# A four-layer streaming encoder on one core: a third output tile's partial products beside the last mixer and the memory job, and a new order of the side products

## The reference: what is computed

```python
h = _rmsnorm(x, norm_g[i])
u = h @ (w_in_a, w_in_b, w_in_c)[kind][j]
mix_u, mq, gate = u[..., :n_mix], u[..., n_mix:n_mix + MEM_W], u[..., n_mix + MEM_W:]
br, st = _mixer_a(...)   # or _mixer_b, _mixer_c
mo = _mem_attend(mq, mem_k[i], mem_v[i])
y = jnp.concatenate([br, mo], axis=-1) * jax.nn.silu(gate)
x = x + y @ w_out[i]
```

## Time and profile before

| | |
|---|---|
| median of three runs | 2914.63 us (2906.01 to 2914.76) |
| the profiled execution | 2914.56 us, span 2912.8 us |
| instructions | 46710, of them 18936 matmuls |
| TensorE busy with matmuls | 2741.2 us |
| its weight loads, beside them | 2572.5 us |
| VectorE and ScalarE | 1322.6 and 1320.6 us |
| GpSimd | 733.3 us |
| mean granted clock of TensorE | 0.971 of full speed |

### The profile page before, as it was taken

How to read it: one execution, slowest core, us unless ns; L and a number is a source line. 1 busy time by engine, 2 the same in 40 slices (tenths; PEclk the granted TensorE clock), 3 DMA queues, 4 the chain that set the end, 5 groups by cost and what they waited for, 6 DMA issues and landing times.

```text
span 2912.8 us, 46710 instructions
## 1 busy us (share of the span) xinstructions
PE 2741.2 (94%) x18936; PEld 2572.5 (88%) x18936; DVE 1322.6 (45%) x3225; ACT 1320.6 (45%) x2833; POOL 733.3 (25%) x408
## 2 busy tenths in 40 slices
PE   7999999989999999979999989999899999999897
PEld 5989999879989999969999878888799999999886
DVE  4035555563215566664425245555613045555642
ACT  4244444442325555552334356666523244444532
POOL 0222222235122222232521122222051222222313
PEclk9999999999999999989999999999899999999998
DMA  4111111115111121114211000000242111111111
GB/s 150 54 50 54 54 47 47 50 32 185 61 40 63 56 70 52 59 39 149 81 59 39 25 27 12 11 12 3 76 147 68 47 47 47 57 47 46 56 68 74
DMA packets 58629, 171.98 MB, mean 59 GB/s; under 512 B 6768, under 2 KB 15472, under 8 KB 57904
## 3 DMA queue, kind: packets, MB, share of 16 engines
q1 hardware_dynamic: 58416, 169.01, 16.8%
HBM read 135.06 MB, written 33.92 MB: 58 GB/s over the span
## 4 chain that ended last, share of the span: by engine, by line
PE 79%; ACT 9%; DVE 8%; issue 3%; DMA 0%; POOL 0%; SPq 0%; DVEq 0%; ACTq 0%
PE acc L1849 39%; PE acc L1939 10%; PE acc L1797 7%; PE turned L1898 6%; PE scores L1882 5%; PE scores L1730 4%; ACT prob L1243 4%; PE turned L1730 2%; PE scores L1871 2%; DVE prob L1534 2%; PE scores L1706 1%; DVE pt_split L1563 1%; DVE y_sb L1592 1%; ACT pt_split L1255 1%; ACT prob L1246 1%
## 5 line engine op out<-in xcount | busy, mean ns | idle before, releaser
L1849 PE MATMUL acc<-h_split,w_hi 128*128 128x352 f32 (+2 forms) x5112 | 960.6, 330 | 28.7 <-ACT w_rest L1096 14.3
L1849 PEld LDWEIGHTS acc<-h_split,w_hi 128*128 128x128 f32 x5112 | 835.0, 191 | 59.2 <-ACT w_rest L1096 16.9
L1628 POOL TENSOR_TENSOR w_lo<-w_raw,w_hi 128x1024 fp32r<-128x1024 f32 (+2 forms) x154 | 333.6, 2168 | 1559.5 <-ACT w_hi L1149 1559.5
L1563 DVE TENSOR_TENSOR pt_split<-turned,pt_split 128x512 fp32r<-128x512 f32 (+4 forms) x564 | 303.2, 552 | 552.4 <-ACT pt_split L1255 551.7
L1534 DVE CUSTOM_DVE_ANT_0 prob<-scores,bias 128x256 f32<-128x256 f32 (+9 forms) x576 | 338.4, 633 | 416.6 <-PE scores L1882 390.8
L1939 PE MATMUL acc<-pt_split,v_split 128*64 128x256 f32 (+5 forms) x3486 | 479.0, 273 | 25.9 <-ACT pt_split L1255 8.0
L1849 PE MATMUL acc<-h_split,w_lo 128*128 128x352 f32 (+2 forms) x2556 | 495.5, 324 | 0.0
L1243 ACT ACTIVATE prob<-prob,stat 128x256 f32<-128x256 f32 (+9 forms) x468 | 303.7, 650 | 305.7 <-DVE stat L1534 305.7
L1939 PEld LDWEIGHTS acc<-pt_split,v_split 128*64 128x64 f32 (+1 forms) x3486 | 389.1, 154 | 42.1 <-ACT pt_split L1255 15.5
L1849 PEld LDWEIGHTS acc<-h_split,w_lo 128*128 128x128 f32 x2556 | 426.0, 190 | 0.0
L1255 ACT ACTIVATE pt_split<-turned 128x512 fp32r<-128x512 f32 (+4 forms) x564 | 261.7, 482 | 242.4 <-PE turned L1898 241.4
(11 more groups left out here) (142 smaller groups left out, 2818.9 us busy)
## 6 DMA issues: line engine op xcount, KB each, us to landing
w_raw<-w SPq DMA_DIRECT2D x132, 512.0 KB, 3.7
x_scr<-y_sb SPq DMA_DIRECT2D x24, 528.0 KB, 5.5
y_sb<-x_scr SPq DMA_DIRECT2D x24, 528.0 KB, 9.1
y_sb<-x_in SPq DMA_DIRECT2D x16, 528.0 KB, 11.7
mw_raw<-w SPq DMA_DIRECT2D x16, 512.0 KB, 9.2
bias<-rel_in SPq DMA_DIRECT2D x24, 320.0 KB, 4.2
raw<-kcache SPq DMA_DIRECT2D x18, 256.0 KB, 3.9
v_cache<-vcache SPq DMA_DIRECT2D x18, 256.0 KB, 3.9
```

What stands on the lines that cost most here:

```text
L1563: ins = dve.tensor_tensor(pt[0:rows, chunk.p % 2, 1, c0:c0 + n], t_ps[chunk.a % 2][0:rows, c0:c0 + n], pt[0:rows, chunk.p % 2, 0, c0:c0 + ...
L1628: pool.tensor_tensor(w_lo[:, n % 2, 0:wide], w_raw[:, n % 2, 0:wide], w_hi[:, n % 2, 0:wide].bitcast(F32), ALU.subtract).then_inc(wlo_made ...
L1849: ins = pe.matmul(acc[s.bank][:, 0:s.cols], w[ws][:, 128 * k:128 * k + 128], x(xs, k), start=(k, y) == products[0], stop=(k, y) == product ...
```

## The change

- **First memory job of layers 0, 1 and 3.** Two of the first mixer's query sides, not none, stand before the first transposes (`ahead` 2), and the five units get 1, 1, 2, 2, 1 of the other seven sides (`BESIDE_FIRST`), where it was 2, 1, 3, 2, 1.
- **Last mixer of A and B.** The three memory-query sides stand in the units as 1, 0, 2, 0, 0 (`BESIDE_LAST`), where it was 1, 1, 1, 0, 0.
- **Output tiles.** Three of them, not two, get partial sums (`OUT_FIRST`), so nine thirds. Two of these stand already in the last mixer's decoded unit, the other seven as 2, 1, 1, 2, 1 (A) or 1, 2, 1, 2, 1 (B) in the memory job's five units. The first tile's thirds leave out k tiles 5 and 7, so 18 matmuls; those of the others leave out 7. Inside a third all high-half activations of the k tiles come first, then the low ones; tile 5's products come last.
- **Tails.** The missing products (5 and 7 for the first tile, 7 for the others) are made from four slots, filled by ScalarE from `w_hi` and `w_lo` (`tailcopy`, both halves) behind the last third of each tile. GpSimd's subtraction for them goes. `before_last` has nine groups instead of six.
- **Gated tiles' copies.** In the last mixer, tiles 6 and 0 are copied in its fourth unit, behind the first transposes; 1 in chunk 2 of that unit; 2 and 3 in its decoded unit, behind the first transposes; 4 behind the memory job's first normalisation. Tile 4's low half is VectorE's now.
- **Output phase.** The pair are tiles 3 and 4; it waits for each weight where it is used first, and begins with all passes of the first weight. Squares 0 and 1 stand before the next weights' splits. `outtile` is left for 5, 6 and 7; the next layer's memory preparation stands behind 5 (one quarter) and 6 (two quarters).
- **Latent mixers' short unit** (two chunks, three sides): one side stands in chunk 0 and two in chunk 1, where it was two and one. Chunk 1's transposes and the second tile of the next unit's scores stand between.

```diff
+BESIDE_LAST = (1, 0, 2, 0, 0)
+
+BESIDE_FIRST = (1, 1, 2, 2, 1)
+
...
-OUT_POOL = (6, 0, 1, 2, 3, 4)
-
-OUT_PARTS = {"A": (1, 1, 1, 2, 1), "B": (0, 2, 1, 2, 1)}
+OUT_POOL = (6, 0, 1, 2, 3)
+
+OUT_PARTS = {"A": (0, 0, 0, 0, 2, 2, 1, 1, 2, 1), "B": (0, 0, 0, 0, 2, 1, 2, 1, 2, 1)}
+
+OUT_FIRST = 3
+
+TAILS = ((5, 7), (7,), (7,))
+TAIL_SLOTS = {(0, 5): 0, (0, 7): 1, (1, 7): 2, (2, 7): 3}
...
     def out_sides(self, layer, weights):
-        return [self.side(w, KT - 1, "opart", a, cols, f, layer, c, 3, 1)
+        return [self.side(w, KT - len(TAILS[f]), "opart", a, cols, f, layer, c, 3, 1)
                 for f, w in enumerate(weights) for c, (a, cols) in enumerate(THIRDS)]
...
+        if s.what == "opart" and part == parts - 1 and s.chunk == s.chunks - 1:
+            self.order.append(("tailcopy", s))
...
             if nxt.kind == "M" and j.kind != "M":
-                count, ahead = (count[0] + ahead, *count[1:]), 0
+                count, ahead = BESIDE_LAST, 0
+            if j.kind == "M" and nxt.kind in "AB":
+                count, ahead = BESIDE_FIRST, 2
...
-        ahead = 2 if gates else AHEAD[jobs[1].kind]
+        ahead = 2 if out or gates else AHEAD[jobs[1].kind]
...
-            if out and u.job is jobs[-1]:
-                if u is u.job.units[0]:
-                    listed = self.out_sides(u.job.layer, out)
-                count, at = OUT_PARTS[KINDS[u.job.layer]], u.job.units.index(u)
-                sides = listed[sum(count[:at]):sum(count[:at + 1])]
+            if out and i >= len(units) - 10:
+                count, at = OUT_PARTS[KINDS[u.job.layer]], i - len(units) + 10
+                if at == 4:
+                    parts_of_out = self.out_sides(u.job.layer, out)
+                if at >= 4:
+                    sides = parts_of_out[sum(count[:at]):sum(count[:at + 1])]
...
-            if out and u is jobs[-2].units[2]:
-                self.early_y(u.job.layer, (6, 0))
-            if out and u is jobs[-2].units[3]:
-                self.early_y(u.job.layer, (1, 2))
-            if out and u is jobs[-2].units[4]:
-                self.early_y(u.job.layer, (3, 4))
...
+            if k < OUT_FIRST:
...
+        early = {}
+        if out and job is jobs[-2]:
+            early = {3: {2: (1,)}}.get(at, {})
...
+            if n == 2 and len(sides) == 3 and job.kind == "C":
+                parts[i > 0].append((s, 0, 1))
+                continue
...
+                if out and job is jobs[-2] and at >= 3:
+                    self.early_y(job.layer, (6, 0) if at == 3 else (2, 3))
...
+                if out and job is jobs[-2] and at == 4:
+                    self.early_y(job.layer, (4,))
...
+            self.early_y(job.layer, early.get(c, ()))
...
-            p.stream(memory[:1] + mixers + memory[1:], out=x["out"][:2])
+            p.stream(memory[:1] + mixers + memory[1:], out=x["out"][:OUT_FIRST])
...
-        first = 0 if kind == "C" else 2
+        first = 0 if kind == "C" else OUT_FIRST
         p.phase("out", layer=layer, weights=x["out"], first=first)
+        p.order += [("square", layer, f) for f in range(min(first, 2))]
         p.used(*x["out"][first:first + 2])
-        p.order += [("square", layer, f) for f in range(first + 2)]
+        p.order += [("square", layer, f) for f in range(min(first, 2), first + 2)]
...
             p.order.append(("square", layer, f))
-            t = f - 3 if first else f - 2
-            if t < 4 and layer < DEPTH - 1:
-                p.order += [("msplit", layer + 1, t), ("mnorm", layer + 1, 2 * t), ("mnorm", layer + 1, 2 * t + 1)]
+            for t in {5: (1,), 6: (2, 3)}.get(f, ()) if first else (f - 2,):
+                if t < 4 and layer < DEPTH - 1:
+                    p.order += [("msplit", layer + 1, t), ("mnorm", layer + 1, 2 * t), ("mnorm", layer + 1, 2 * t + 1)]
...
+    wt_hi = sbuf("w_tail_hi", [4, 128], F32R, at=qo_at)
+    wt_lo = sbuf("w_tail_lo", [4, 128], F32R, at=qo_at + 2048)
...
+                    act.wait_ge(*tail_made.upto(n - 2))
...
-                if n in tail_weights:
-                    act.activation(wt_hi[:, tail_weights[n], :], w_raw[:, n % 2, 128 * (KT - 1):128 * KT],
-                                   ACT.Copy).then_inc(tail_hi.mark(n), 1)
...
+            elif name == "tailcopy":
+                s = item[1]
+                act.wait_ge(*operand_lo.upto(plan.last_job[s.job].n, 1))
+                act.wait_ge(*whi_made.upto(s.weight))
+                act.wait_ge(*wlo_made.upto(s.weight))
+                for k in TAILS[s.dst]:
+                    slot, cols = TAIL_SLOTS[s.dst, k], slice(128 * k, 128 * k + 128)
+                    act.activation(wt_hi[:, slot, :], w_hi[:, s.weight % 2, cols].bitcast(F32), ACT.Copy).then_inc(
+                        tail_made.mark(s.weight), 1)
+                    act.activation(wt_lo[:, slot, :], w_lo[:, s.weight % 2, cols].bitcast(F32), ACT.Copy).then_inc(
+                        tail_made.mark(s.weight), 1)
...
-                if n in tail_weights:
-                    f, tail = tail_weights[n], slice(128 * (KT - 1), 128 * KT)
-                    pool.wait_ge(*tail_hi.upto(n))
-                    pool.tensor_tensor(wt_lo[:, f, :], w_raw[:, n % 2, tail], wt_hi[:, f, :].bitcast(F32),
-                                       ALU.subtract).then_inc(tail_lo.mark(n), 1)
...
-            for w in weights:
-                pe.wait_ge(*whi_made.upto(w))
             passes = ((0, 0), (1, 0), (0, 1))
             for k in ks:
                 if k == ks[-1] and before_last is not None:
                     before_last()
                 pe.wait_ge(*hi_ready(k))
                 listed = [(y, i) for y in range(3) for i in range(2)]
-                if k == ks[-1]:
-                    pe.wait_ge(*lo_ready(k))
+                if k == ks[-1] or k == ks[0] and before_last is not None:
                     listed.sort(key=lambda yi: yi[1])
                 for y, i in listed:
                     (ws, xs), w = passes[y], weights[i]
                     if xs == 1 and i == 0:
                         pe.wait_ge(*lo_ready(k))
+                    if k == ks[0] and y == 0:
+                        pe.wait_ge(*whi_made.upto(w))
                     if ws == 1 and k == ks[0]:
                         pe.wait_ge(*wlo_made.upto(w))
...
-                        pe.wait_ge(*tail_lo.upto(more["weights"][1]))
-                        for f in range(2):
+                        pe.wait_ge(*tail_made.upto(more["weights"][first - 1]))
+                        for f in range(first):
...
+                                products = [(k, y) for k in TAILS[f] for y in range(3)]
+                                for k, y in products:
+                                    ws, xs = PASSES[y]
+                                    ins = pe.matmul(acc[i % 2][:, 0:n], (wt_hi, wt_lo)[ws][:, TAIL_SLOTS[f, k], :],
+                                                    h_v[:, xs, k, a:a + n], start=(k, y) == products[0],
+                                                    stop=(k, y) == products[-1])
...
+                    if KINDS[layer] != "C" and f == OUT_FIRST + 2 and c < 2:
+                        pe.wait_ge(*out_added.upto(layer, OUT_FIRST - 1, 1 + c))
...
-                    products = [(k, y) for k in OUT_ORDER["A"][:-1] for y in range(3)]
+                    products = [(k, y) for ys in ((0, 2), (1,)) for k in OUT_ORDER["A"] if k not in (5, 7) for y in ys]
+                    products += [(5, y) for y in range(3) if s.k_tiles == KT - 1]
...
-                    if s.what == "opart" and s.chunk == s.dst == 0:
+                    if s.what == "opart" and s.chunk == 0 and (s.dst == 0 or k == 5):
```

10 lines of the change are left out of this document (1 added, 9 removed).

## The result

The changed kernel takes 2896.98 us (median of ten runs, 2893.3 to 2902.8), the kernel before 2913.49 (ten runs, 2906.0 to 2917.2). The ratio is 0.9949, with a 95% interval of 0.9939 to 0.9958. It is faster by 16.5 us; 34.4 were forecast. The profiled execution (2902.8 us) is the slowest of its ten, so its span shows only 11.8 us less than that of before.

A forecast was written before the change was run, and what follows sets the result against it. TensorE was taken as the bound, so only its waits and granted clock could move time: waits -20.4 and clock -14 took 2914.56 to 2880 us, range 2858 to 2897.

The forecast's parts named there:

- First memory jobs: Layers 0, 1 and 3: two query sides fill TensorE's 6.05 us wait, -16.9 us of waits and -9 of clock.
- Short units: Five latent short units: 2.64 us wait goes, a 1.6 us wait for VectorE comes; -7.5 us, and -2 of clock.
- rival B: Clock gives nothing back, the low stretches only stand elsewhere: 2894 us; chance 0.17.
- Ends of layers 0, 1 and 3: Last mixer and memory job: +3 us each in layers 0 and 3, -3.5 in layer 1, -3 of clock in all.
- moving the copies buys nothing: Layer ends: the second output weight's split holds ScalarE as long as the two copies did, so moving them gains nothing.
- The rule: A VectorE instruction with two SBUF inputs waits out a GpSimd one reading SBUF; for tile 4's low half, 2.4 us per layer.
- rival C: Short unit gains 0 and VectorE is held once more in each layer end (+7 us): 2896 us; chance 0.1.
- Output phase: Start -0.5 us a layer (-1.5); GpSimd's later memory preparation +1.5 in each of layers 0 and 1 (+3).
- D: Output sides before the decoded unit's V product wait for late tile copies, holding everything behind: 2917 us or more; chance 0.03.
- D's sign: The decoded unit's V product starting over 20 us after the scores before it would show the forecast wrong.

The follow-up runs named there:

- run 1: The kernel before with only the first memory jobs changed (two query sides ahead, then 1, 1, 2, 2, 1): 2884.4 us, ratio 0.9905.
- run 2: The kernel before with only the latent jobs' short unit changed: 2900.3 us, ratio 0.9958.
- run 12: run 3 plus only the gated tiles' copies in their new places, tile 4's low half on VectorE: 2878.1 us.
- Runs 5: The changed kernel with memory quarters 1 and 2 prepared behind output tile 5 and quarter 3 behind 6: 2896.3 us.
- 6: The kernel before with the changed kernel's place for the memory quarters (1 behind output tile 5, 2 and 3 behind 6): 2914.8 us, ratio 1.0008.
- run 9: The changed kernel with two memory quarters prepared ahead of the output phase, behind tile 7's copy, quarter 2 behind tile 5, 3 behind 6: 2887.7 us.
- run 8: The changed kernel with no output sides in the last mixer's decoded unit, 2, 2, 1, 2, 2 in the memory job's units: 2888.2 us.
- 10: The changed kernel with both the early memory preparation and no output side in the decoded unit: 2876.6 us, ratio 0.9876.
- 13: The changed kernel with early memory preparation, no decoded-unit output side, and gated tiles' copies in their old places, tile 4's low half on GpSimd: 2871.4 us.
- run 14: The changed kernel with early memory preparation, no decoded-unit output side, old copy places, and memory-query sides as 1, 1, 1, 0, 0 again: 2867.5 us.
- run 3: The kernel before with the first memory jobs and the short unit both changed, nothing of the output part: 2873.0 us, ratio 0.9866.
- run 4: The changed kernel with the memory tokens' low halves on VectorE instead of GpSimd: 2923.1 us, ratio 1.0038.
- run 7: The changed kernel with memory tokens' low halves on VectorE, placed behind the additions of the next output tile: 2911.0 us, ratio 1.0000.

## Why the prediction was right and wrong

**First memory jobs: right.** Forecast -16.9 of waits and -9 of clock, -25.9. The three stretches are 8.0, 8.1 and 7.1 us shorter, -23.2, and the waits in them 16.0 us; run 1 alone gives -28.2. So the clock gave 7.2 us in that profile, where 9 were forecast. The wait went, 0.61 stayed, the clock is at 1.00.

**Short units: right.** Forecast -9.5; the five mixers are 10.7 us shorter, run 2 gives -12.3. The new wait has the place, the releaser and the length (1.51 for 1.6) of the working. That the clock would stay low beside a smaller wait (rival B) did not come: the window has 1.00.

**Ends of layers 0, 1 and 3: waits near, clock wrong.** With the 8.7 us of moved matmuls taken off, +4.0, -2.1 and +4.4 us against the forecast's +3, -3.5 and +3. TensorE's waits in them changed by +3.3, -0.4 and +2.3 us, so layer 1's waits did not shrink as forecast. The 3 us of clock that I took back there did not come: the windows have 0.90 and 0.91, where 0.91 and 0.87 were, and what layer 1 gains by it the longer windows of layers 0 and 3 lose again. The wait for tile 4's copy is where it was expected, 1.96 us for the working's 2.9. The sentence that moving the copies buys nothing should have gone one step further: run 12 shows that it costs 5 us. I had the rows for it: GpSimd's low halves now run beside the decoded unit's and the memory job's multiplies. I applied this price to tile 4's low half alone, where it did not fall due (1.25 us), and not to the normalisations that the other copies moved next to. The rule's rival C named the right mechanism at the wrong instruction.

**Output phase: wrong, and the largest error.** The step "GpSimd ended them at 729.84 for use at 732.06; now one more weight's low half (2.4) and two small ones (1.4) stand there too", priced at +1.5 in each of layers 0 and 1 with bounds 0 and +4, failed. With the moved matmuls added back, the stretches are 6.9 and 6.2 us longer; the run from tile 7's end to the pair is 5.2 and 5.4 longer, outside the bounds. Of the 5.2, 3.56 are the wait for GpSimd and 1.6 the clock, 0.92 for 1.00 over 20.2 us, for which the step had no term. I compared the row's tail and took its start as unchanged. But an output tile of 11.6 us had left the stretch, with one weight's low half (2.4), while all squares and the whole preparation stayed: 38.5 us are left to GpSimd's row where it had 46.0. And it stands idle for 25.12 us just ahead of it, since the plan lists the preparation behind the pair's squares. Runs 5 and 6 speak against the order of the quarters, which is what my step had blamed; run 9, with two quarters ahead of the stretch, has no wait and the stretch of 15.1 us that the kernel before had.

**The sum.** Two edits -39.6 (forecast -35.4), the output part +24 (forecast about +1: +6 - 3.5 - 3 for the ends and their clock, -1.5 + 3 for the output phase). Of these 24, memory preparation is 9 to 12 (runs 9; 8 against 10), sides in the decoded unit 9 to 11 (runs 8; 9 against 10), copies 5 (runs 12; 10 against 13). These were single removals, so the shares needn't add up exactly; with the preparation early, no side in the decoded unit, and the copies and the sides' order as before, run 14's median is below run 3's, within the scatter of both. The changed kernel is slower than its first edit alone (run 1, 2884.4).

**Rivals.** D was right in kind for the decoded unit: the output sides there do hold the V product, which starts 14.4 us after the scores before it (603.69 and 618.13; D's sign was 20), and what is behind it. But that costs 9 to 11 us in all three layers together (runs 8 and 10), not the 34 that it would have needed. B's 2894 is near the measured time by another way: the clock came back where the waits went, and the waits grew elsewhere. So that 2896.98 is still inside the stated range, whose end of 2897 was set for B and C, is luck.

## What to carry to other kernels

When work leaves a stretch, list what stays in it on every other engine and compare the new length with their whole row, not with the row's last slack; the engine that was at 25% over the kernel can be at 100% there. Time each part of a bundled change alone: here two simple edits gave 39.6 us and the third, larger part took 24 of them back. Work that must be ready later belongs where its engine idles, even if a whole phase earlier, and ahead of items that would make it wait in the queue.

## What the runs showed of the hardware

Some of VectorE's instructions grow with what GpSimd does beside them: a scaling of 128x256 takes 0.47 us alone (run 4) and 2.04 on average in run 7's four (8.17 us), a low half of the same size 0.38 and 2.06, a multiply 0.35 and 2.52. Not all do: the reduction of scores of 128x256 takes 0.42 us in the changed kernel both beside GpSimd's low halves (604.85) and where GpSimd is idle (622.92). TensorE's clock can be low in a stretch without a wait of its own: the decoded unit of run 8 is busy throughout and has 0.66, behind a unit with three waits of 1.28 to 2.39 us and 0.69 (their windows, in this order, below), while the first memory job has 1.00 with its one wait of 0.61 us.

```profile
601.70:608.40 6.70, 6.70 (x65) 6.04 (x64) 4.34 (x15) 4.96 (x13) 4.48 (x3) 0.66 0.28 84
586.80:601.70 14.90, 9.80 (x65) 8.16 (x63) 8.58 (x14) 10.12 (x17) 13.20 (x7) 0.69 0.29 84
```
